# Order of loads at the end of a feed-forward stage, and of three steps at the head of a mixture of experts

## The reference, cut to what matters

```python
def layer_norm(x, g, b):
    xf = x.astype(jnp.float32)
    mean = jnp.mean(xf, axis=-1, keepdims=True)
    var = jnp.mean(jnp.square(xf - mean), axis=-1, keepdims=True)
    return ((xf - mean) * lax.rsqrt(var + LN_EPS) * g + b).astype(x.dtype)

def swiglu(h, w1, w3, w2):                  # layer 0: D 1024, D_FF 2816
    return (jax.nn.silu(h @ w1) * (h @ w3)) @ w2

def moe_swiglu(h, router_w, router_b, w1, w3, w2):   # layer 1: 8 experts of 1408, top 2
    logits = (h @ router_w).astype(jnp.float32) + router_b.astype(jnp.float32)
    top_logit, top_idx = lax.top_k(logits, TOP_K)
    top_p = jax.nn.softmax(top_logit, axis=-1)
    gates = jnp.einsum('btk,btke->bte', top_p,
                       jax.nn.one_hot(top_idx, N_EXPERTS, dtype=jnp.float32)).astype(h.dtype)
    y = jnp.zeros_like(h)
    for e in range(N_EXPERTS):
        y = y + gates[..., e:e + 1] * swiglu(h, w1[e], w3[e], w2[e])
    return y

# second block, per layer: the modulation whose weights travel beside layer 0's feed-forward
        mod = (c_act @ w_ada[layer] + b_ada[layer])[:, None, :]
```

## Time and profile before

| | us |
|---|---|
| median of three runs | 2984.96 |
| the profiled execution itself | 2984.97 |
| its span (first to last instruction) | 2983.3 |
| PE busy | 2799.4 (94%) |
| DVE busy | 1876.9 (63%) |
| ACT busy | 1422.8 (48%) |
| POOL busy | 453.2 (15%) |
| mean granted TensorE clock, share of full | 0.983 |

### The profile page before, as it was taken

The page is one execution under the profiler, slowest core; times in us unless marked ns, Lnnn a source line. Parts: engine busy times, 40 slices in busy tenths (PEclk is TensorE's granted clock), DMA queues, the critical chain, the costliest instruction groups (busy, mean ns, idle before and its releaser), DMA issues. The chain is left out here.

```text
span 2983.3 us, 63798 instructions
## 1 busy us (share of the span) xinstructions
PE 2799.4 (94%) x27233; PEld 2303.6 (77%) x27233; DVE 1876.9 (63%) x3037; ACT 1422.8 (48%) x2227; POOL 453.2 (15%) x434
## 2 busy tenths in 40 slices
PE   7899999999899899999889999999989999999999
PEld 2795677777778667787549999999975756678877
DVE  4852565565665358765768888888866157376652
ACT  1212556665664242221337777777754246243331
POOL 1003345655552010000010000000010010000000
PEclk9999999999999999999989999999999999999999
DMA  5454000000000277755239999999962210222232
GB/s 213 166 208 147 31 22 22 22 22 22 3 3 4 85 270 280 279 199 207 90 140 394 379 367 370 364 371 367 370 239 80 91 65 20 100 80 91 98 113 71
DMA packets 73846, 482.17 MB, mean 162 GB/s; under 512 B 11107, under 2 KB 13027, under 8 KB 32144
## 3 DMA queue, kind: packets, MB, share of 16 engines
q1 hardware_dynamic: 59360, 418.48, 37.1%
q0 software_dynamic: 11952, 51.91, 4.7%
q10 hardware_dynamic: 2304, 8.39, 0.7%
HBM read 457.20 MB, written 34.13 MB: 165 GB/s over the span
## 5 line engine op out<-in xcount | busy, mean ns | idle before, releaser
L2425 DVE TENSOR_TENSOR sb_moe_w_lo<-w_ring,sb_moe_w_hi 128x1408 fp32r<-128x1408 f32 (+1 forms) x132 | 255.1, 1933 | 69.4 <-ACT sb_moe_w_hi L2370 67.5
L2273 PE MATMUL ps<-sb_moe_w_hi,sb_x_feat_lo 128*128 128x352 f32 x832 | 273.5, 329 | 5.3 <-DVE sb_moe_w_lo L2425 5.2
L2275 PE MATMUL ps<-sb_moe_w_hi,sb_x_feat_hi 128*128 128x352 f32 x832 | 267.7, 322 | 0.0
L2274 PE MATMUL ps<-sb_moe_w_lo,sb_x_feat_hi 128*128 128x352 f32 x832 | 266.9, 321 | 0.0
L2370 ACT ACTIVATE sb_moe_w_hi<-w_ring 128x2816 fp32r<-128x2816 f32 x80 | 204.2, 2553 | 2.6 <-DMA w_ring<-w_moe_up 1.8
L2273 PE MATMUL ps<-sb_moe_w_hi,sb_hid_feat_lo 128*128 128x256 f32 x572 | 163.2, 285 | 3.9 <-DVE sb_hid_feat_lo L2556 3.9
L2273 PEld LDWEIGHTS ps<-sb_moe_w_hi,sb_x_feat_lo 128*128 128x128 f32 x832 | 156.1, 188 | 11.9 <-issue 11.1
L2275 PE MATMUL ps<-sb_moe_w_hi,sb_hid_feat_hi 128*128 128x256 f32 x572 | 161.9, 283 | 0.0
L2274 PE MATMUL ps<-sb_moe_w_lo,sb_hid_feat_hi 128*128 128x256 f32 x572 | 161.8, 283 | 0.0
L1445 PE MATMUL ps<-sb_tb,w_ring 64*64 64x64 f32 x3840 | 141.2, 219 | 17.3 <-ACT sb_tb L1612 16.1
L2274 PEld LDWEIGHTS ps<-sb_moe_w_lo,sb_x_feat_hi 128*128 128x128 f32 x832 | 157.0, 189 | 0.0
(11 more groups left out here) (553 smaller groups left out, 7570.7 us busy)
## 6 DMA issues: line engine op xcount, KB each, us to landing
w_ring<-w_moe_up SPq DMA_DIRECT2D x67, 1408.0 KB, 8.6
sb_hm<-w_ada SPq DMA_DIRECT2D x48, 1024.0 KB, 6.9
w_ring<-w_ffn SPq DMA_DIRECT2D x22, 1024.0 KB, 4.8
w_ring<-w_up SPq DMA_DIRECT2D x22, 1024.0 KB, 4.8
sb_b_again<-w_moe_up SPq DMA_DIRECT2D x13, 1408.0 KB, 8.2
sb_hm<-w_moe_up SPq DMA_DIRECT2D x13, 1408.0 KB, 8.2
sb_t_again<-w_moe_up SPq DMA_DIRECT2D x13, 1408.0 KB, 8.1
w_ring<-w_moe_down SPq DMA_DIRECT2D x13, 1408.0 KB, 7.7
```

Source lines behind the costliest of these rows:

```text
L2273: pe.matmul(out, x_lo, w_hi, start=first, stop=False)
L2274: pe.matmul(out, x_hi, w_lo, start=False, stop=False)
L2275: return pe.matmul(out, x_hi, w_hi, start=False, stop=end)
L2425: return V.tensor_tensor(WL[:, s, w], raw[raw_at(c, i)[0]][:, w], WH[:, s, w].bitcast(F32), ALU.subtract)
```

## The change

SP's list in the feed-forward puts down chunk m+1 ahead of the loads of modulation tile 15+m+1, where it stood behind them. In `Norm`, ACT takes the root before `weights()`; DVE's `rest(0, 0)` moves out of the norm to the place behind the subtraction of the greatest logit. TensorE does eight fillers before the row numbers instead of two before and three behind. The logits are computed in four groups of output partitions, a quarter (32 of each 128) of the tokens in each, 128 columns a product; a 32x32 block transpose on DVE replaces the copy and TensorE's turn.

```diff
--- before.py
+++ after.py
@@ -443,9 +443,9 @@
         for k in range(KT):
             act.wait_ge(dve_m.sem, dve_m.at(f"c{k}"))
             S.activation(self.SQ[:, k, :], src[:, k, :], ACT.Square).then_inc(*act_m.did(f"q{k}"))
-        weights()
         act.wait_ge(self.pe_m.sem, self.pe_m.at("var"))
         S.activation(self.R[:, 0:P], self.k.ps[:, 7, 0:P], ACT.Sqrt, bias=self.k.tiny[:, 0:1]).then_inc(*act_m.did("root"))
+        weights()
         for k in range(KT):
             act.wait_ge(dve_m.sem, dve_m.at(f"n{k}"))
             S.activation(self.k.X[:, k, :], src[:, k, :], ACT.Identity, bias=self.beta[:, k:k + 1],
@@ -1920,8 +1920,9 @@
                             sp.wait_ge(self.s_lo, self.parted + KT)
                         if 6 <= c < 6 + UP:
                             ada_load(sp, c - 6)
-                        if c >= FT:
-                            ada_load(sp, UP + c - FT)
+                        if c > FT:
+                            ada_load(sp, UP + c - FT - 1)
+                    ada_load(sp, NB - 1)
 
                 @block.gpsimd
                 def _(pool):
@@ -2141,7 +2142,7 @@
                                           "past", "of", "held", "capped", "items", "later", "later128", "base", "over", "row", "jump",
                                           "moved", "ra0", "ra1", "rb0", "rb1", "rows",
                                           "num", "den", "rec", "gate", "ga0", "ga1", "gb0", "gates"])
-        s_exp, s_number, s_lt = self.sem("router_exp"), self.sem("row_numbers"), self.sem("logits_turned")
+        s_exp, s_number = self.sem("router_exp"), self.sem("row_numbers")
         V, S = nc.vector, nc.scalar
         UP, DOWN = FE // HCOL, D // YCOL
         ROUND = UP + DOWN
@@ -2274,13 +2275,15 @@
                         pe.matmul(out, x_hi, w_lo, start=False, stop=False)
                         return pe.matmul(out, x_hi, w_hi, start=False, stop=end)
 
-                    whole.tensor(pe, 2)
+                    whole.tensor(pe, 8)
                     pe.wait_ge(s_rc, 80)
                     pe.matmul(ps[:, 6, 0:P], self.con("ones"), before[:, :], start=True, stop=True).then_inc(s_number, 1)
-                    self.keep_warm(pe, 0, 3)
                     for k in range(KT):
                         pe.wait_ge(whole.dve_m.sem, whole.dve_m.at(f"h{k}"))
-                        last = pe.matmul(ps[0:NE, 4, :], rw[:, k * NE:(k + 1) * NE], H[:, k, :], start=(k == 0), stop=(k == KT - 1))
+                        for g in range(4):
+                            last = pe.matmul(ps[32 * g:32 * g + NE, 4, 0:P].rearrange("p (a n) -> p a n", n=32), rw[:, k * NE:(k + 1) * NE],
+                                             H[:, k, :].rearrange("p (a g n) -> p a g n", g=4, n=32)[:, :, g, :],
+                                             start=(k == 0), stop=(k == KT - 1))
                     last.then_inc(s_l, 1)
 
                     for t in range(TT):
@@ -2292,12 +2295,6 @@
                                 last = pe.transpose(ps[:, n % 4, k * P:(k + 1) * P], H[:, 4 * g + k, t * P:(t + 1) * P],
                                                     self.con("id"))
                             last.then_inc(s_tr, 1)
-                            if n == 1:
-                                pe.wait_ge(route.sem, route.at("flat"))
-                                for u in range(TT):
-                                    last = pe.matmul(ps[:, 6, u * NE:(u + 1) * NE], flat[0:NE, u * P:(u + 1) * P],
-                                                     self.con("id")[0:NE, 0:NE], start=True, stop=True)
-                                last.then_inc(s_lt, 1)
 
                     pe.wait_ge(route.sem, route.at("sel"))
                     for t in range(TT):
@@ -2443,13 +2440,13 @@
 
                     did = route.did
                     full = [P, TT, NE, NE]
-                    whole.vector(dve, lambda: rest(0, 0))
+                    whole.vector(dve, lambda: None)
                     dve.wait_ge(s_number, 1)
                     V.tensor_copy(number, ps[:, 6, 0:P]).then_inc(*did("number"))
                     dve.wait_ge(s_l, 1)
-                    V.tensor_copy(flat[0:NE, :], ps[0:NE, 4, :]).then_inc(*did("flat"))
-                    dve.wait_ge(s_lt, 1)
-                    V.tensor_tensor(L[:, :, :], ps[:, 6, 0:TT * NE].rearrange("p (t e) -> p t e", e=NE),
+                    V.transpose(flat[:, 0:P], ps[:, 4, 0:P]).then_inc(*did("flat"))
+                    mine("flat")
+                    V.tensor_tensor(L[:, :, :], flat[:, 0:P].rearrange("p (t n) -> p t n", n=32)[:, :, 0:NE],
                                     rb[:, :].unsqueeze(1).broadcast_to([P, TT, NE]), ALU.add).then_inc(*did("lg"))
                     mine("lg")
                     other = L[:, :, :].unsqueeze(2).broadcast_to(full)
@@ -2473,6 +2470,7 @@
                     V.tensor_tensor(Z[:, :, :], L[:, :, :], mx[:, :, 0:1].broadcast_to([P, TT, NE]),
                                     ALU.subtract).then_inc(*did("shift"))
 
+                    rest(0, 0)
                     dve.wait_ge(s_pre, 1)
                     V.tensor_copy(row[:, :, :], ps[:, 7, 0:TT * NE].rearrange("p (t e) -> p t e", e=NE)).then_inc(*did("pre"))
                     V.tensor_copy(cnt[:, :], ps[:, 7, TT * NE:(TT + 1) * NE]).then_inc(*did("cnt"))
```

## The result

Seven runs of the changed kernel took 2972.58 us (median), 2965.93 to 2975.67; seven of the kernel before took 2986.29 (2981.73 to 2993.4). The ratio is 0.995 (95% interval 0.9937 to 0.9963), 11 to 19 us faster. The profiled execution took 2971.2 us, its span 2969.6, with a granted clock of 0.980; before it was 2984.97, 2983.3 and 0.983.

What follows compares the result with a forecast made beforehand. TensorE was taken to set the pace, with movable waits in the down chunks and the experts' head: 11.9 + 6.4 = 18.3 us off 2984.97 gives 2966.7 us, range 2962.5 to 2973.2 for 8 in 10.

Steps and rivals of the forecast that it cites:

- rival A: Down chunks gain, the experts' head does not (near ties, or half clock through the eight fillers): 2973.1 us, chance 0.11.
- Down chunks: Feed-forward down chunks: no TensorE wait left, 15.57 us a turn, 11.9 us gained; DVE keeps 4.2 us of slack.
- Rival B: Head gains, down chunks only a third, since TensorE waits for DVE and not the weights: 2974.6 us, chance 0.07.
- D: Slower: modulation halves land late behind a whole chunk on SP and DVE waits; 3013 us at 20 us landings, chance 0.02.
- E: No effect: SP's wait for the freed ring buffer holds the chunk until the old time; 2985 us, chance 0.02.
- Spread: Experts' head: spread starts 2.7 us earlier, held by TensorE's fillers, not the 3.3 us by which DVE is earlier.
- Logits: Experts' head: eight four-column groups at 0.36 us take 2.9 us; by the skill's rule 1.7 us.
- Rival C: Logit groups do not overlap, 7.0 us instead of 2.9, so half the head's gain: 2970.8 us, chance 0.10.
- Transposes: Experts' head: 32 transposes on TensorE take 4.1 us, and the prefixes' products start behind them at 1540.6.
- From the prefixes to the gather: Experts' head: the half-clock spell before the gather was expected again, with everything shifting by 6.4 us.
- Rest of chunk 0: Experts' head: DVE's moved rest ends before the prefixes come, leaving 1.1 us of cover; uncovered it costs up to 3.09 us.
- everything behind just starts sooner: Up chunks and expert loop: a microsecond taken out ahead of either is not given back inside it.

Runs made afterwards that it cites:

- the two comparisons: Changed kernel against the kernel before, timed twice: 2972.58 against 2986.29 us, ratio 0.995; then 2970.99 against 2987.15 us, ratio 0.9945.
- the added steps: Changed kernel with six, then sixteen, extra DVE instructions in each down turn, results unread: 2974.32 and 2993.39 us, one run each.
- the order alone: Changed kernel with the old fillers, logits and turn, keeping SP's new order, the earlier root and the later rest of chunk 0: 2970.0 us, one run.
- the chunks' part: Kernel before with only SP's new order of loads in the feed-forward; measured alone 2979.96 us, ratio 0.9975.

## Why the prediction was right, and where its sizes were off

The time, 2972.58, lies in the range of 2962.5 to 2973.2, near its upper end, and the sign was right. The forecast of 2966.7 took 18.3 us off one profiled execution; the two comparisons gave 11 to 19 and 11 to 22. That the time fell inside the range owes something to luck. Two errors of opposite sign met: the head gave 3.5 us more than forecast, and about 8 us went missing in stages that the sum left at nothing. With the forecast's head the same losses would have ended near 2976. The measured time is also that of rival A to about half a microsecond, whose reason did not apply. The range's lower bound does not come out of the terms named for it: 2964.5 less 1.2 is 2963.3, not 2962.5.

*Down chunks: right.* -11.9 was forecast, -11.6 to -11.9 measured in every trace with the change and without added work (194.2 against 205.8 to 206.0), a turn of 15.55 us against 15.57. That TensorE would find no new wait rested on DVE's slack of 4.2 us; the added steps gave 3.7 on average and 4.1 to 4.7 in the later turns. Rival B (DVE is the bound) has fallen with that, and so has D: from the second pair on the halves are issued 9 us or more after the chunk ahead of them, and DVE has no wait for them. E fell with SP's list.

*Spread: right.* It starts 2.13 us behind the start of the fillers instead of 4.83: -2.7, as forecast, bound by the fillers and not by the reciprocal.

*Logits: the mis-sized term.* Forecast 2.9 us (eight groups of 0.36), measured 1528.52 - 1526.65 = 1.87, 3.7 times faster than the 6.97 before. The 0.36 was read from a single group between wide products; eight groups in a row took 0.23 each. That a changeover on either side of the single group makes the difference fits this but was not tested, since that group also had 32 output rows and not 8. The Trainium skill, "TensorEngine Tiling (Array Packing)", Theoretical Speedup, says up to 4x: this trace comes close to it with 3.7x, and the prediction's estimate from it, 1.7 us, was better than the row's. Rival C (groups one after another) fell.

*Transposes: 0.6 too long.* 3.55 us for 32 back to back; 4.1 was read from pieces with the turn of the logits between them.

*From the prefixes to the gather: 1.5 too long.* 5.68 us instead of 7.20. The forecast let the spell of half clock recur at the same place. It came, but later. By windows of 1 us the clock before fell at about 1549.7, 2.6 us behind the first prefix product; after, it fell 4 us behind it:

```profile
1535.00:1536.00 1.00, 1.00 (x5) 0.58 (x5) 0.92 (x5) 0.00 (x0) 0.00 (x0) 1.00 0.95 406
1536.00:1537.00 1.00, 1.00 (x3) 0.43 (x2) 0.93 (x6) 0.00 (x0) 0.00 (x0) 0.53 0.98 414
```

The columns are those of the earlier trace rows, the seventh number the clock. So the last prefixes (1.31 us in the trace with the order alone, 0.89 here) and part of the fillers ran at full clock. This piece is not the change's doing for certain: from the first prefix product to the first expert product the unchanged kernel took 17.38 us in one trace and 15.74 in the other, and the changed one 15.71.

*Rest of chunk 0: a tie.* DVE finished it at 1535.22 and copied the prefixes at 1535.29; TensorE's last prefix product ended at about the same time. Of the cover of 1.1 us nothing was left: the prefixes came 3.2 us behind their products' start instead of 3.8, and the rest began 0.4 later against it. It cost nothing here, but a further gain on TensorE in front of it would meet DVE's rest.

So the head gave 9.9 where 6.4 were forecast: 1.0 of the 3.5 from the logits, 0.6 from the transposes, 1.5 from the gather's fillers, 0.15 behind it, the rest is small pieces. Rival A fell too.

*The whole: less than its parts.* 21.8 us were gained locally, and 13.7 to 16.2 were measured between the medians. The step that did not hold is that "everything behind just starts sooner". It held inside the chunks. It did not hold for the norms between, whose length depends on where the half clock falls: 50.2, 54.6 or 56.1 us for the pool's, 85.9 to 90.9 behind the loop. The prediction priced one spell, before the gather, and took the others as fixed. The profile of before has a short stage behind the loop (85.9, where half of the later traces have 90.3 or more), and its runs lie 12 to 16 us apart, as much as the gain. That the missing time lies in the norms is read from the table, and the kernel without fillers in the sums fits it: its pool norm and pool took 50.1 us although its clock was at half there, and it was 10 to 12 us faster than the changed kernel. It does not prove it, since that edit also shortens a step at full clock, from 0.78 to 0.60 us.

*Open:* why the spells fall where they do, and whether the changed program itself moves them. The entry of the feed-forward, which lies ahead of everything changed, took 200.3 us in the traces without the chunks' part (three of three), and 200.3 to 205.4 in those with it (three of eleven at 200.3). Only the kernel before and the changed one have a second trace, and the changed one's two are alike. If the change moves the spells, part of its gain is given back in every execution. If they fall by chance, the medians should differ by the whole local gain; by the marks above that is 21 to 24 us, at or beyond the upper ends of the two intervals (19 and 22). That leans to the first reading, but no run here separates the two.

## What to carry to other kernels

Check a local gain between two marks that both traces share before comparing the whole; if untouched stages move as well, run the old kernel a second time and see whether they move there. A filler that is meant to keep TensorE's clock up must still fit into the gap at half clock: where ScalarE delivers a step every 0.6 us and the step with its filler takes 0.78 at full and 1.31 at half clock, the filler becomes the bound. And price a new form of product by a row with the same neighbours: a lone group between other forms read 0.36 us, and eight in a row 0.23 each.

## What the runs showed of the hardware

Half-clock stretches of 10 to 14 us came at different places in two executions of an unchanged program, with TensorE busy all through them: over 12 us of the pool's norm the granted clock was 0.57 in one trace of the kernel before and 1.00 in the other. One such stretch cost 3 to 6 us in a norm (entry 203.6 against 200.3, pool 54.6 and 56.1 against 50.2).

Four column groups of 8 output rows, each 32 partitions apart, run nearly four at a time when many follow each other: 1.87 us against 6.97 for the same columns in wide products. A single group of the same length between wide products, with 32 output rows, took 0.36 us, against 0.23 a group in the row of eight.
